# Retention and sparse-attention block: two element-wise steps of attention on GpSimd, VectorE's queue reordered, and a last stage pipelined over tiles

## The reference, cut to what matters

```python
y_ret = retention(rq, rk, rv)            # 4 heads of 128; each head RMS-normed over its 128 columns
y_ret = y_ret * silu(rg)                 # the retention gate
y_nsa = g0 * o_cmp + g1 * o_sel + g2 * o_win      # three gated attention branches, 8 heads of 64
x = x + ga1 * (concat([y_ret, y_nsa]) @ w_out)
h2 = rmsnorm(x, g) * (1 + sc2) + sh2
x = x + ga2 * ((silu(h2 @ w_ff_gate) * (h2 @ w_ff_up)) @ w_ff_down)
return rmsnorm(x, ln_final_g)            # y * rsqrt(mean(y*y) + eps) * g
```

## Time and profile before

| | us |
|---|---|
| three runs: median (lowest, highest) | 727.98 (725.49, 729.76) |
| profiled execution: its own time | 729.54 |
| its span, first to last instruction | 727.7 |
| TensorE busy in the span | 682.1 |
| VectorE busy | 332.8 |
| ScalarE busy | 225.5 |
| GpSimd busy | 265.9 |

### The profile page before, as it was taken

The page is one execution under the profiler, slowest core; times in us unless marked ns, Lnnn a source line. Parts: engine busy times, 40 slices in busy tenths (PEclk is TensorE's granted clock), DMA queues, the critical chain, the costliest instruction groups (busy, mean ns, idle before and its releaser), DMA issues.

```text
span 727.7 us, 9019 instructions
## 1 busy us (share of the span) xinstructions
PE 682.1 (94%) x3547; PEld 564.1 (78%) x3547; DVE 332.8 (46%) x587; ACT 225.5 (31%) x378; POOL 265.9 (37%) x127
## 2 busy tenths in 40 slices
PE   2678899999989898999999999999999999999995
PEld 1556679987768687888898888888888888888884
DVE  4878999977465668152620110000000029633126
ACT  4435233422132333332542222222222213232222
POOL 2316443432000111138034434434434427545531
PEclk9699999999998899999999999999999999999999
DMA  9975986665000000176014233233233223232002
GB/s 314 359 257 152 353 293 234 199 240 228 30 2 1 0 2 1 40 221 202 1 48 127 87 96 107 87 98 104 87 102 101 89 86 117 86 103 72 0 1 116
DMA packets 73962, 88.09 MB, mean 121 GB/s; under 512 B 3048, under 2 KB 57536, under 8 KB 73792
## 3 DMA queue, kind: packets, MB, share of 16 engines
q1 hardware_dynamic: 73184, 86.36, 36.0%
q0 software_dynamic: 416, 1.08, 0.4%
q10 hardware_dynamic: 320, 0.07, 0.0%
HBM read 85.41 MB, written 2.10 MB: 120 GB/s over the span
## 4 chain that ended last, share of the span: by engine, by line
PE 78%; DVE 10%; ACT 3%; issue 3%; DMA 3%; SPq 2%; POOL 0%; POOLq 0%; DVEq 0%
PE ps L1523 11%; PE ps L1524 11%; PE ps L1522 11%; PE ps L1141 11%; PE ps L1143 11%; PE ps L1142 11%; PE ps L1274 3%; DMA raw<-in_w_in 3%; DVE acc L732 2%; DVE ps L875 1%; SPq L344 1%; PE ps L1332 1%; PE ps L1399 1%; PE ps L1228 1%; ACT hf L488 1%
## 5 line engine op out<-in xcount | busy, mean ns | idle before, releaser
L404 POOL TENSOR_TENSOR wl<-raw,wh 128x1024 fp32r<-128x1024 f32 (+1 forms) x94 | 238.6, 2543 | 285.8 <-ACT wh L456 285.6
L456 ACT ACTIVATE wh<-raw 128x1024 fp32r<-128x1024 f32 (+1 forms) x94 | 97.4, 1039 | 154.4 <-PE ps L1524 73.9
L1522 PE MATMUL ps<-hTh,wh 128*128 128x512 f32 (+1 forms) x384 | 142.8, 372 | 0.0
L1523 PE MATMUL ps<-hTl,wh 128*128 128x512 f32 (+1 forms) x384 | 142.6, 371 | 0.0
L1524 PE MATMUL ps<-hTh,wl 128*128 128x512 f32 (+1 forms) x384 | 142.6, 371 | 0.0
L1106 DVE TENSOR_TENSOR act<-ps,sg 128x512 f32<-128x512 f32 x22 | 15.2, 692 | 212.3 <-PE ps L1524 212.3
L1141 PE MATMUL ps<-wh,hTh 128*128 128x512 f32 (+1 forms) x224 | 90.5, 404 | 11.8 <-DVE hTl L770 10.6
L1143 PE MATMUL ps<-wh,hTl 128*128 128x512 f32 (+1 forms) x224 | 85.8, 383 | 0.0
L1142 PE MATMUL ps<-wl,hTh 128*128 128x512 f32 (+1 forms) x224 | 85.7, 383 | 0.0
L1522 PEld LDWEIGHTS ps<-hTh,wh 128*128 128x128 f32 x384 | 72.4, 188 | 12.5
L1523 PEld LDWEIGHTS ps<-hTl,wh 128*128 128x128 f32 x384 | 72.4, 188 | 12.4
(11 more groups left out here) (197 smaller groups left out, 818.4 us busy)
## 6 DMA issues: line engine op xcount, KB each, us to landing
raw<-in_w_ada SPq DMA_DIRECT2D x32, 512.0 KB, 5.8
raw<-in_w_ff_gate SPq DMA_DIRECT2D x22, 512.0 KB, 3.8
raw<-in_w_ff_up SPq DMA_DIRECT2D x22, 512.0 KB, 3.7
raw<-in_w_ff_down SPq DMA_DIRECT2D x22, 512.0 KB, 3.2
raw<-in_w_in SPq DMA_DIRECT2D x20, 512.0 KB, 7.0
early<-in_w_ada SPq DMA_DIRECT2D x16, 512.0 KB, 9.6
raw<-in_w_out SPq DMA_DIRECT2D x8, 512.0 KB, 6.6
xs<-in_x SPq DMA_DIRECT2D x4, 512.0 KB, 5.3
```

The lines of the kernel that those rows point to most:

```text
L404: pool.tensor_tensor(lo, raw[:, slot, 0:n], hi.bitcast(F32), ALU.subtract).then_inc(w_lo, 1)
L456: a.activation(split(u, n)[0], raw[:, slot, 0:n], ACT.Copy).then_inc(w_hi, 1)
L1522: mm(o, hi[:, ks], hTh[:, k, c0:c1], start=k == 0, stop=False)
L1523: mm(o, hi[:, ks], hTl[:, k, c0:c1], start=False, stop=False)
```

## The change

Four edits. (1) `add_branch`'s last operation, the addition into `mix`, goes to GpSimd; VectorE's next write of `tmpo` waits for it. (2) `ret_norm` is halved: VectorE writes the normed tile to free space in `hTf` (the factor 0.5 is folded into the variance), signals `r_half`, and GpSimd multiplies by `rg` and signals `r_norm`; TensorE's `cmp_values` of tiles 2 and 3 waits for `r_half`. (3) In VectorE's slots `add_branch` stands first, ahead of `row_min` and `max_rows`; `cmp_gates(1)` stands between the row minima of group 3; `OUT_AT` goes from slots 16, 20, 26, 30 to 14, 18, 31, 33. GpSimd gets a slot loop of its own. (4) The last stage is pipelined: the finish of a tile comes after the first half of the next one, the last tile's second half is cut into two pieces of 256 columns, ScalarE scales and sends the upper 512 columns of every tile on its own queue, and VectorE and SyncE the lower 512.

```diff
+HALF = D // 2
+PIECES = [[(0, HALF), (HALF, D)]] * (TT - 1) + [[(0, HALF), (HALF, 768), (768, D)]]
-OUT_AT = {16: 0, 20: 1, 26: 2, 30: 3}
+OUT_AT = {14: 0, 18: 1, 31: 2, 33: 3}
...
+        def normed_y(i):
+            tok = max(i, TT - 2) * P
+            return hTf[:, 0, 0:RH, tok:tok + P]
+        def piece_count(t, n):
+            return 2 * t + n + 1
...
@@ sync
-                sp.dma_start(out[t * P:(t + 1) * P, :], xb[:, t % 2, :]).then_inc(out_done[t], 16)
+                sp.dma_start(out[t * P:(t + 1) * P, 0:HALF], xb[:, t % 2, 0:HALF]).then_inc(out_done[t], 16)
...
@@ gpsimd
+            def add_branch(x):
+                i, b = divmod(x, 2)
+                pool.wait_ge(o_read, x + 1)
+                pool.wait_ge(c_mix, i + 1)
+                y = mix[:, i % 2, 512:1024]
+                pool.tensor_tensor(y, y, tmpo[:, :], ALU.add).then_inc(b_mix, 1)
+                pool.wait_ge(b_mix, x + 1)
+            def ret_gate(i):
+                pool.wait_ge(r_half, i + 1)
+                pool.tensor_tensor(mix[:, i % 2, 0:512].rearrange("p (h x) -> p h x", h=RH), normed_y(i),
+                                   rg[:, i, :].rearrange("p (h x) -> p h x", h=RH), ALU.mult).then_inc(r_norm, 1)
+            def attention():
+                for n in range(SLOTS):
+                    if n % 2 and n // 2 in STEP0[1:]:
+                        add_branch(STEP0.index(n // 2) - 1)
+                    if n in SQ_AT:
+                        power(N_RET + SQ_AT[n], yss[:, :])
+                    if n in NORM_AT:
+                        ret_gate(NORM_AT[n])
+                    if n in OUT_AT:
+                        low(U0_OUT + OUT_AT[n])
...
@@ scalar
+            def finish(t):
+                a.wait_ge(y_scaled, piece_count(t, len(PIECES[t]) - 1))
+                a.wait_ge(rstd_ok, N_X2 + t)
+                a.activation(xb[:, t % 2, HALF:D], xb[:, t % 2, HALF:D], ACT.Copy, scale=rstd[:, t:t + 1]).then_inc(y_high, 1)
+                a.wait_ge(y_high, t + 1)
+                a.dma_start(out[t * P:(t + 1) * P, HALF:D], xb[:, t % 2, HALF:D]).then_inc(out_done[t], 16)
+                for n, (c0, c1) in enumerate(PIECES[t]):
+                    a.wait_ge(x2_ok, piece_count(t, n))
+                    if t and n == 0:
+                        a.wait_ge(var_ok, N_X2 + t - 1)
+                    a.activation(sqj[...], x1[:, t, c0:c1], ACT.Square, accum_out=part[:, n:n + 1]).then_inc(sq3, 1)
+                    if t and n == 0:
+                        finish(t - 1)
+            finish(TT - 1)
...
@@ vector, add_branch
+                if x:
+                    d.wait_ge(b_mix, x)
                 d.tensor_tensor(tmpo[...], o[...], r[...], ALU.mult).then_inc(o_read, 1)
-                d.wait_ge(o_read, x + 1)
-                d.wait_ge(c_mix, i + 1)
-                y = mix[:, i % 2, 512:1024]
-                d.tensor_tensor(y, y, tmpo[:, :], ALU.add).then_inc(b_mix, 1)
-                d.wait_ge(b_mix, x + 1)
@@ vector, ret_norm
-                then(d.tensor_tensor(heads_view(tmpo[:, :], RH), heads_view(ps[:, 7, :], RH), yss[...], ALU.mult))
-                d.scalar_tensor_tensor(mix[:, i % 2, 0:512], tmpo[:, :], 0.5, rg[:, i, :], ALU.mult, ALU.mult).then_inc(r_norm, 1)
-                d.wait_ge(r_norm, i + 1)
+                if i:
+                    d.wait_ge(r_norm, i)
+                d.tensor_tensor(normed_y(i), heads_view(ps[:, 7, :], RH), yss[...], ALU.mult).then_inc(r_half, 1)
@@ vector, slots
-            for h in range(HPG):
-                row_min(3, h)
+            row_min(3, 0)
+            row_min(3, 1)
             cmp_gates(1)
+            row_min(3, 2)
+            row_min(3, 3)
             for n in range(SLOTS):
+                if n % 2 and n // 2 in STEP0[1:]:
+                    add_branch(STEP0.index(n // 2) - 1)
                 for x, h in PAIR_AT.get(n, []):
                     row_min(x, h)
                 if n in MAX_AT:
                     max_rows(MAX_AT[n])
-                if n % 2 and n // 2 in STEP0[1:]:
-                    add_branch(STEP0.index(n // 2) - 1)
...
@@ vector, last stage
+            def take(t, n):           # x1 piece += PSUM piece, signals x2_ok
+            def scale_final(t, n):    # xb piece = x1 piece * gfin piece, signals y_scaled;
+                ...                   # for t >= 2 and n == 0 first: d.wait_ge(out_done[t - 2], 32)
+            def variance_final(t, n): # rstd column (+)= part[:, n] / D (+ EPS)
+            def finish(t):
+                d.wait_ge(rstd_ok, N_X2 + t)
+                d.wait_ge(y_scaled, piece_count(t, 0))
+                d.tensor_scalar(xb[:, t % 2, 0:HALF], xb[:, t % 2, 0:HALF], rstd[:, t:t + 1], None, ALU.mult).then_inc(y_ok, 1)
             for t in range(TT):
+                last = len(PIECES[t]) - 1
+                take(t, 0)
+                scale_final(t, 0)
+                if t:
+                    finish(t - 1)
+                then(variance_final(t, 0))
+                for n in range(1, last + 1):
+                    take(t, n)
+                for n in range(1, last + 1):
+                    if n == last and last > 1:
+                        then(variance_final(t, 1))
+                    scale_final(t, n)
+                variance_final(t, last).then_inc(var_ok, 1)
+            finish(TT - 1)
...
@@ tensor, cmp_values
-                    pe.wait_ge(r_norm, i)
+                    pe.wait_ge(r_half, i)
```

More of the change, by code:

```diff
@@ L207, in block_kernel @@
         ssq = small("ssq", [P, TT])
-        ssq2 = small("ssq2", [P, TT])
+        part = small("part", [P, 3])
         rstd = small("rstd", [P, TT])
@@ L263, in block_kernel @@
         mx_ps, mx_min, mx_T, mb_ok, st_ps, p_exp, pv, o_read = (sem(n) for n in ("mx_ps", "mx_min", "mx_T", "mb_ok", "st_ps", "p_exp", "pv", "o_read"))
-        c_mix, b_mix, v_ones, mcol_set, masks_in = (sem(n) for n in ("c_mix", "b_mix", "v_ones", "mcol_set", "masks_in"))
+        r_half, c_mix, b_mix, v_ones, mcol_set, masks_in = (sem(n) for n in ("r_half", "c_mix", "b_mix", "v_ones", "mcol_set", "masks_in"))
         cs_ps, c_pre, c_exp, c_den, c_T, cT_ok, c_o = (sem(n) for n in ("cs_ps", "c_pre", "c_exp", "c_den", "c_T", "cT_ok", "c_o"))
@@ L270, in block_kernel @@
         gate_ps, up_ps, sg_ok, act_ok, a_hi, a_lo, a_used = (sem(n) for n in ("gate_ps", "up_ps", "sg_ok", "act_ok", "a_hi", "a_lo", "a_used"))
-        d_ps, x2_ok, sq3, y_ok = (sem(n) for n in ("d_ps", "x2_ok", "sq3", "y_ok"))
+        d_ps, x2_ok, sq3, y_ok, y_high = (sem(n) for n in ("d_ps", "x2_ok", "sq3", "y_ok", "y_high"))
         gates_ok = sem("gates_ok")
@@ L378, in _ @@
                 sp.wait_ge(y_ok, t + 1)
-                sp.dma_start(out[t * P:(t + 1) * P, :], xb[:, t % 2, :]).then_inc(out_done[t], 16)
+                sp.dma_start(out[t * P:(t + 1) * P, 0:HALF], xb[:, t % 2, 0:HALF]).then_inc(out_done[t], 16)
             for t in range(TT):
-                sp.wait_ge(out_done[t], 16)
+                sp.wait_ge(out_done[t], 32)
         @block.gpsimd
@@ L414, in _ @@
             for u in range(UNITS):
-                for i in {U0_OUT: (0, 1), U0_OUT + 2: (2,), U0_OUT + 4: (3,)}.get(u, ()):
-                    power(N_RET + i, yss[:, :])
+                if u == U0_OUT:
+                    attention()
+                if U0_OUT <= u < U0_OUT + len(OUT_AT):
+                    continue
                 if u == U0_GU + SPLIT:
@@ L682, in _ @@
                 high(U0_DOWN + f)
-            for t in range(TT):
[L684 to L690, removed]
+            def finish(t):
[4 more added lines that the diff above has]
+                a.dma_start(out[t * P:(t + 1) * P, HALF:D], xb[:, t % 2, HALF:D]).then_inc(out_done[t], 16)
+            for t in range(TT):
+                for n, (c0, c1) in enumerate(PIECES[t]):
+                    a.wait_ge(x2_ok, piece_count(t, n))
+                    if t and n == 0:
+                        a.wait_ge(var_ok, N_X2 + t - 1)
+                    a.activation(sqj[:, c0 % HALF:c0 % HALF + c1 - c0], x1[:, t, c0:c1], ACT.Square, accum_out=part[:, n:n + 1]).then_inc(sq3, 1)
+                    if t and n == 0:
+                        finish(t - 1)
+            finish(TT - 1)
         @block.vector
@@ L943, in ret_var @@
                 d.wait_ge(r_sq, i + 1)
-                d.tensor_scalar(yss[:, :], yss[:, :], 1.0 / RDV, EPS, ALU.mult, ALU.add).then_inc(var_ok, 1)
+                d.tensor_scalar(yss[:, :], yss[:, :], 4.0 / RDV, 4.0 * EPS, ALU.mult, ALU.add).then_inc(var_ok, 1)
             def ret_norm(i):
                 d.wait_ge(rstd_ok, N_RET + i)
-                then(d.tensor_tensor(heads_view(tmpo[:, :], RH), heads_view(ps[:, 7, :], RH),
-                                     yss[:, :].unsqueeze(2).broadcast_to([P, RH, RDV]), ALU.mult))
-                d.scalar_tensor_tensor(mix[:, i % 2, 0:512], tmpo[:, :], 0.5, rg[:, i, :], ALU.mult, ALU.mult).then_inc(r_norm, 1)
-                d.wait_ge(r_norm, i + 1)
+                if i:
```

(21 more changed lines are left out.)

## The result

The changed kernel is slower: 735.17 us in the median of five runs (733.28 to 737.18) against 726.88 for the kernel before on the same chip, a ratio of 1.0107 with a 95% interval of 1.0076 to 1.0138, that is 7.8 us more. The profiled execution has a span of 735.4 us where the kernel before had 727.7.

A forecast was written before the change was run, and what follows sets the result against it. TensorE was taken as the bound (78% of the chain), with VectorE ending its pauses and setting the tail. Attention 1.2 plus tail 2.1 gave 3.3 us off 727.98, forecast 724.7 us, range 720.8 to 728.3.

The forecast's parts named there:

- the paragraph on the port: GpSimd's shared port in attention: contention would touch only VectorE's `scale_unit`s, and no sum changes.
- place A: Slots 3 to 7, `add_branch` put first: values of group 2 start earlier, gain 0.45 us.
- place C: Slots 24 to 27: pauses before `cmp_values(3)` and `pair(7,2)` shrink or go, gain 1.5 us.
- Place D: Slots 32 and 33: a `scale_unit` ahead of `add_branch(6)` delays the values of group 7, cost 1.15 us, pause 1.55.
- one more fall of the clock: Rival: one more 7 us stretch near 1.2 GHz, behind the pause before group 7's values: 728.1 us, chance 0.12.
- The number of falls: TensorE's clock in attention: as many falls as before; a 7 us stretch at 0.51 costs 3.4 us.
- Place B: Slots 13 to 15: `cmp_values(2)` is released by `r_half` at about 244.1, not 244.54, gain 0.4 us.
- The tail: After TensorE's last matmul: the pipelined last stage ends at 722.5 where it was 724.58, gain 2.1 us.
- The rival of late transfers: Last stage: ScalarE's output transfers take 4.8 us, not 2.6, giving 729.1 us; chance 0.07.
- GpSimd's operations: Twelve operations on 128x512 moved to GpSimd in attention, taken as 1.2 us each, between 0.92 and 1.40.
- The rival on the slower side: Late ScalarE transfers in the last stage, 729.1 us, chance 0.07; measurably slower needs a clock fall too, 0.03.

The follow-up runs named there:

- the filler: Seven unused 512-column matmuls added before the values of group 7: 731.93 us in the changed kernel, 724.09 in the one with the old order.
- the old order: The changed kernel with `add_branch` back behind `row_min` and `max_rows`, `OUT_AT` 14, 18, 31, 33 kept: 725.81 us, ratio 0.9984 to the kernel before.
- the tail alone: The kernel before with only the pipelined last stage, attention as before: 723.67 us, ratio 0.9942 to the kernel before.
- the moves alone: The changed kernel with VectorE's order and `OUT_AT` as before, leaving the two operations on GpSimd and the new tail: 719.91 us, ratio 0.9897.
- both repairs: The changed kernel with the gate multiplication reading one SBUF input and the fourth output unit in slot 35: 720.66 us, ratio 0.9900.
- repairing the hold alone: The changed kernel with the reciprocal written to PSUM, so the gate multiplication reads one SBUF input: 731.12 us, ratio 1.0034.
- moving the scaling alone: The changed kernel with the fourth output unit in slot 35 instead of 33, its scaling behind `add_branch(6)`: 730.56 us, ratio 1.0020.
- attention alone: The changed kernel with the last stage as before, so only the attention edits: 738.53 us, ratio 1.0146 to the kernel before.
- one SBUF input: The changed kernel with the reciprocal in PSUM, so the 128x8 gate multiplication reads one SBUF operand: 731.12 us, ratio 1.0034.
- the best version: Operations on GpSimd, order as before, gate multiplication with one SBUF input, `OUT_AT` 16, 20, 31, 35, new tail: 719.70 us, ratio 0.9886.

## Why the prediction was wrong

- **The contention was looked at and dismissed.** The step that failed is the paragraph on the port: "Here that would touch only the `scale_unit`s among what is left on VectorE in attention ... and no sum changes". I had checked the large operations and passed over L895, a multiplication of 128x8 that stands in the middle of `add_branch`, has two SBUF inputs, and takes part in every chain that I summed (the 0.20 in 1.13). The Trainium skill (GPSIMD Engine Reference, section "Key points") names the kind of VectorE instruction, two SBUF inputs, and no size. The trace agrees beside the retention gate and the low part, where 0.17 became 0.97, 2.08 and 1.15, and it does not beside GpSimd's power of 128x4, where 0.17 stayed. The `scale_unit` of slot 13 that I did name took 1.58 in place of 1.22 beside GpSimd's addition (244.23), and the paragraph put that at nothing. The held multiplication is why place A lost 0.5 where I forecast a gain of 0.45, why place C gained 0.5 and not 1.5, and why slot 19 to 20, for which I had no place at all, lost 4.6 with the fall of the clock at its pause.
- **Place D was right and its price was not.** The pause was forecast as 1.55 and is 1.52; the scaling of 1.22 stands between `ret_var(3)` and the reciprocal as described. But I priced it at 1.15 in the sum and gave one more fall of the clock a chance of 0.12 at 3.4 us. The fall came, and cost 5.2 us in the profile and 3.9 in the runs with the filler. In the kernel with the old order, timed twelve times, five times are of the group that the filler took away.
- **The number of falls was taken as given.** "I count as many falls as before in the forecast" held the range at 728.3. The change made two pauses of 1.5 and 2.1 us, and in its profile the clock fell at each. The filler shows that one such pause can decide on 4 us.
- **Place B** was forecast at 0.4 and gives 0.35 (a lag of 3.36 us at slot 14, 3.01 at `cmp_values(2)`). The number is right with a scaling 0.36 longer than I took in it.
- **The tail** was forecast at 2.1 and gives 2.6: GpSimd's power took 0.55 where I took 0.92, and the transfers landed in 2.0 us (SyncE's queue) and 2.5 (ScalarE's) where I took 2.6. The rival of late transfers did not happen.
- **GpSimd's operations** were taken as 1.2 and are 1.27. The edits behind them are worth having: in the old order they gain 3.3 us by the runs, more than the 1.2 that I gave them together with the new order; a part of it is falls of the clock that do not come (two in the profile of the tail alone, none in that of the moves alone), which my sum did not have.
- **The rival on the slower side** named the wrong place. None of the rivals had two causes at once, and it took both to reach 735: of the 15 us between the changed kernel and the one with both repairs, repairing the hold alone leaves 9.7 and moving the scaling alone 8.7.

What stays open: why the tail alone gains 1.6 us more in the runs than its profile shows, and why both repairs together give 15 us and not 11.6. The length of the falls scatters from execution to execution, and I have one profile of each kernel. Open as well is why GpSimd's power lets the small multiplication through when the other operations do not.

## What to carry to other kernels

Before work goes to GpSimd, list every VectorE instruction that reads two SBUF tensors and may run at the same time, down to those of 8 columns: each can be held until GpSimd's instruction ends, and one operand in PSUM frees it. Here additions, multiplications and subtractions of 512 to 1024 columns held such instructions, and a power of 128x4 did not. When an instruction is put ahead of a release for which TensorE waits, price the pause with the fall of TensorE's clock that may follow, not with its own length; idle matmuls in the pause tell the two apart. Separate the parts of such a change: here the two moves and the tail were each a gain, and a changed slot table with a changed order turned 1.0% faster into 1.1% slower.

## What the runs showed of the hardware

- The 128x8 multiplication with two SBUF inputs, started under GpSimd's multiplication of 128x512 or subtraction of 128x1024, is not slowed but held to its end: three ends at 218.36, 261.23 and 280.80, against GpSimd's 218.33, 261.20 and 280.78. Sixteen such cases stand in seven profiles, all ending 0.01 to 0.03 behind GpSimd. The same instruction with one input in PSUM takes 0.17 under the same cover.
- Under GpSimd's power of 128x4 the same multiplication with two SBUF inputs takes 0.17, in all ten profiles in which they meet.
- It goes the other way as well. GpSimd's power of slot 32 and VectorE's scaling ran together in the changed kernel, and the power took 1.92 where it takes 1.01 to 1.05 (1.01 in the best version, whose scaling comes later):

```profile
302.87 1.22 DVE L847 TENSOR_TENSOR raw<-raw,ga 128x1024 f32<-128x1024 f32 x1
303.04 1.92 POOL L420 TENSOR_TENSOR yss<-yss,expo 128x4 f32<-128x4 f32 x1 [3.38 <-DVE yss L989]
```

- More work made the kernel faster: seven matmuls whose result nobody reads, 1.7 us from the start of the first to the next instruction, gave 3.9 us back in one kernel, and took the upper group of times away in another.
- The same pause was followed by a fall of the clock in three profiles (1.52 or 1.53 us in the changed kernel, attention alone and one SBUF input) and not in a fourth (1.52 in the old order).
